# Reciprocal square roots of query and key tiles and of the small norms: a power on GpSimd in place of log and exp on ScalarE

## The chip, the core and the metric

The kernel runs on one core of a Trainium2 chip. A core has a matrix engine (TensorE, in the profile PE for matmuls and PEld for weight loads), VectorE (DVE), ScalarE (ACT), GpSimd (POOL) and SyncE (SP, which here issues the DMAs). Each engine runs its own instructions in order and waits on semaphores for the others. The metric is the device time of one execution in microseconds (us).

## The reference

The program is two blocks of two layers each on 512 tokens of width 1024, in float32. The places that matter here are root-mean-square norms:

```python
def rms_norm(x, g):
    xf = x.astype(jnp.float32)
    y = xf * lax.rsqrt(jnp.mean(xf * xf, axis=-1, keepdims=True) + EPS)   # EPS = 1e-6
    return (y * g.astype(jnp.float32)).astype(x.dtype)

# first block, each layer: L = 16 meta tokens + 512 tokens, 16 query heads, 2 key/value heads of 64
h = rms_norm(x, norm_g)
z = h @ w_in                                     # aq, ak, av, ag, mq, mk, mv, mi, mf, mo, mgate
q = rms_norm(aq.reshape(B, L, 16, 64), q_norm_g) # the query and key norms
k = rms_norm(ak.reshape(B, L, 2, 64), k_norm_g)
q, k = apply_partial_rope(q, cos, sin), apply_partial_rope(k, cos, sin)
ya = sliding_window_sink_attention(q, k, v, sink) * silu(ag)
hm = rms_norm(mlstm_chunkwise(...), out_norm_g)  # per head of 256: the small norm "hsc"
y = concatenate([ya, hm * sigmoid(mo) * silu(mgate)]) @ w_out
x = x + y

# second block, each layer
o_a = rmsnorm(diff_attention(...)) * (1.0 - lam_init)   # per head of 128: "dnorm"
mem_n = rmsnorm(mem, g_mem)                             # "memprep"
...
return rmsnorm(x, g_final)                              # after both layers: "final"
```

## The kernel before

Activations are held transposed, channels on the 128 partitions and the 528 (first block) or 512 tokens along the free dimension. Every projection is a float32 product made of three passes (high x high, high x low, low x high parts). ScalarE rounds each incoming weight piece to its high part (`ch<-st`), VectorE subtracts to get the low part (`cl<-st,ch`).

The order of all work is written out by hand. Class `Order` makes one list of steps (`put(kind, ...)`), and each engine's program walks that list and does its part of every step it knows. So the order of steps in the list is the order of instructions on every engine. Semaphores stand between them: `then_inc(name, keys)` publishes keys, `wait_ge(keys)` waits for them.

The query and key norm is done for nine tiles per layer of the first block, 128 channels (two heads) by 528 tokens each: tile 8 holds the keys, tiles 0 to 7 the queries. A tile goes through these steps:

- projection (`proj`, TensorE), then `qkev` (ScalarE): a copy to the buffer QF and a square to `sq`.
- `qkn`: TensorE multiplies the squares with a block matrix of 1/64, which leaves the mean square of each head on all its partitions (`ps<-sq,cst`). The result lies in the PSUM banks 4 and 5, called P2, which the transposes of the attention probabilities (`sB`, in the profile `ps<-cst,ZR` and `ps<-cst,Z`) use too. ScalarE takes the logarithm with EPS as bias out of P2 into the buffer RS (and so frees P2), then the exponential of -0.5 times it, in place. VectorE scales QF by RS and the gain.
- `rope`: TensorE multiplies QF with the rotation matrix (`ps<-Z,cst`), VectorE multiplies this with the sines, GpSimd multiplies QF with the cosines, VectorE adds both; ScalarE copies the sum into the high part QH, VectorE subtracts to get the low part QL.

`Order.block1` sets where these steps stand. `chain()` puts the `rope` of the tiles in `st["turn"]` and then the `qkn` of those in `st["norm"]`. It is called after a query projection and after each step of filler work. After the keys (8), the values and tiles 0 and 1, the attention loop runs over 32 steps s: scores and softmax `sA(s)`, one unit of filler (`mv`, `cv` or a query projection), `chain()`, transposes `sB(s-1)`, product with the values `sC(s-2)`. Query tiles come in pairs: (2, 3) at s = 4 and 5, (4, 5) at 12 and 13, (6, 7) at 20 and 21; tile t is first needed at s = 4t.

The small norms take a logarithm and an exponential on ScalarE too, over 2 to 32 columns: `hsc` for each of 4 heads per layer (128x5), `memprep` (128x2) and `dnorm` (128x32) once per layer of the second block, `final` (128x4) at the end. The four big norms between the layers (`nrm0`) have the same two functions. ScalarE loads a table before a logarithm and another before the next exponential; copies, squares, tanh and exp go with the latter.

Of the kernel before, what the change touches and what calls it, by code (L numbers as in the profile page):

```python
# [9 lines left out]
ALU = mybir.AluOpType  # L10
ACT = mybir.ActivationFunctionType
X = mybir.AxisListType.X

L = 528
ZC = 25720
NM = 16
EPS = 1e-6
# [11 lines left out]
    ("g1", 8), ("g2", 8), ("gm", 8), ("og", 8), ("qg", 1), ("kg", 1), ("sink", 16), ("cb", 8), ("cw", 32),  # L29
    ("bi", 1), ("bf", 1))]  # L30
DERIVED = [(f"{n}_{l}", w) for n, w in (("negsink", 16), ("qg8", 1), ("og4", 8), ("cwh", 32), ("cbh", 8))
           for l in range(2)] + [("lam", 4), ("eps", 1)]
ENGINES = ("pe", "dve", "act", "pool")


# [101 lines left out]
def v2(ap):  # L137
    return ap.rearrange("p (a b) -> p a b", a=2)
# [131 lines left out]
class Order:  # L270
# [6 lines left out]
    def put(self, *step):  # L277
        self.o.append(step)
# [79 lines left out]
    def block1(self, l):  # L358
# [9 lines left out]

        def chain():

            for t in st["turn"]:
                put("rope", l, t, self.nsq())
            st["turn"] = []
            for t, s in st["norm"]:
                put("qkn", l, t, s)
                st["turn"].append(t)
            st["norm"] = []

        def qk(t, u):
            self.proj(("q", l, t), nid, L, u, t % 2)  # L380
# [371 lines left out]
def program(nc, I, out):  # L752
    with ExitStack() as ctx:
# [50 lines left out]
        def tok(key, T):  # L804
            return ps2(key)[:, :, 0:HALF] if T == L else ps1(key)[:, 0:T]
# [12 lines left out]
        def P(name, i=0, n=1, p=128):  # L818
            return par[0:p, place[name] + i:place[name] + i + n]
# [581 lines left out]
        def scalar_program(act):  # L1401
# [55 lines left out]
            def qkn(l, t, n):  # L1457
                key, rs = ("n", ("qkn", l, t)), RS[t % 3]
                act.wait_ge(("full", key), ("ones",))
                act.activation(v2(rs), tok(key, L), ACT.Ln, bias=P("eps")).then_inc("act_qkn", ("free", key))  # L1460
                act.wait_ge(("free", key))
                act.activation(rs, rs, ACT.Exp, scale=-0.5).then_inc("act_qkn", ("rs", l, t))

            def rope(l, t, n):
                if t < 8:
# [131 lines left out]
                act.wait_ge(("full", key), *sqw(n))  # L1597
                act.activation(v2(sq[n % 2]), tok(key, L), ACT.Tanh, scale=0.5).then_inc("act_tanh", ("ggt", l, k))

            def hsc(l, h):  # L1600
                act.wait_ge(("mss", l, h, 4))
                act.activation(ssq[:, :, h], ssq[:, :, h], ACT.Ln, bias=P("eps"), scale=1.0 / 256).then_inc(
                    "act_hsc", ("hs0", l, h))
                act.wait_ge(("hs0", l, h))
                act.activation(ssq[:, :, h], ssq[:, :, h], ACT.Exp, scale=-0.5).then_inc("act_hsc", ("hss", l, h))

            def ys(l, k):
                y, hi, lo = y_of(k)
                act.wait_ge(("yag", l, k) if k < 8 else ("ym", l, k - 8), ("full", ("gg", l, 7)))
# [2 lines left out]
            def memprep(l):  # L1612
                act.wait_ge(("mem", l))
                for a in range(2):
                    m = act.activation(mem_sq[l][:, a, :], mem_in[l][:, a, :], ACT.Square, accum_out=sm[:, a:a + 1])
                m.then_inc("act_mem", ("ms0", l))
                act.wait_ge(("ms0", l))
                act.activation(sm, sm, ACT.Ln, bias=P("eps"), scale=1.0 / 1024).then_inc("act_mem", ("ms1", l))
                act.wait_ge(("ms1", l))
                act.activation(sm, sm, ACT.Exp, scale=-0.5).then_inc("act_mem", ("memr", l))  # L1620

            def memturn(l):
                act.wait_ge(("memt", l))
# [44 lines left out]
            def dC(l, x, n):  # L1668
# [4 lines left out]
                act.activation(sq[n % 2][:, 0:128], ps1(key)[:, 0:128], ACT.Square,  # L1673
                               accum_out=ss[:, 8 * i + h:8 * i + h + 1]).then_inc(
                    "act_do", ("free", key), ("sqfree", n), ("dss", l, x))

            def dnorm(l):
                act.wait_ge(("dss", l, 31))
                act.activation(ss, ss, ACT.Ln, bias=P("eps"), scale=1.0 / 128).then_inc("act_dnorm", ("ds0", l))
                act.wait_ge(("ds0", l))  # L1680
                act.activation(ss, ss, ACT.Exp, scale=-0.5).then_inc("act_dnorm", ("dsr", l))

            def lqev(l, g, x, t):
                if x == 0:
# [122 lines left out]
                    act.activation(osq_tmp[:, 0:n], OT2[:, a, o:o + n], ACT.Square,  # L1807
                                   accum_out=so[:, 4 * k + a:4 * k + a + 1]).then_inc("act_out", ("osq", k, a))

            def final():  # L1810
                act.wait_ge(("so",))
                act.activation(so[:, 8:12], so[:, 8:12], ACT.Ln, bias=P("eps"), scale=1.0 / 1024).then_inc(
                    "act_out", ("so1",))
                act.wait_ge(("so1",))
                act.activation(so[:, 8:12], so[:, 8:12], ACT.Exp, scale=-0.5).then_inc("act_out", ("so2",))

            do = dict(w=w, sqa=sqa, nrm0=nrm0, nrm=nrm, prep=prep, lines=lines, tab=tab, qkev=qkev, qkn=qkn, rope=rope, swap=swap, vev=vev,
                      vtr=vtr, cvev=cvev, conv=conv, mvev=mvev, agev=agev, m_s=m_s, sA=sA, sB=sB, sC=sC, gr=gr,
                      grf=grf, grt=grt, mA=mA, mB=mB, goev=goev, ggev=ggev, hsc=hsc, ys=ys, memprep=memprep,
                      memturn=memturn, kvvev=kvvev, dqkev=dqkev, dvev=dvev, dgev=dgev, dA=dA, dB=dB, dC=dC,  # L1820
                      dnorm=dnorm, lqev=lqev, lvev=lvev, lS=lS, lse0=lse0, mqev=mqev, lse1=lse1, lgev=lgev, eT=eT,
                      eP=eP, yasp=yasp, fA=fA, fB=fB, mgev=mgev, gtev=gtev, ybs=ybs, yms=yms, mgs=mgs, turn=turn,
                      osq=osq, final=final, bar=act.bar)
            for kind, *a in steps:
                if kind in do:
                    do[kind](*a)
# [1 line left out]
        def vector_program(dve):  # L1828
# [4 lines left out]

            def load():
                dve.memset(ones[:, :], 1.0 / 1024)
                dve.memset(P("eps"), EPS).then_inc("dve_ones", ("ones",))

            def xt(k):
# [544 lines left out]
        def gpsimd_program(pool):  # L2383
            def nrm(nid, k, n):
                if k % 2:
                    T = L if nid < 2 else 512
                    pool.wait_ge(("hh", nid, k))
                    pool.tensor_tensor(hl[:, k, 0:T], sq[n % 2][:, 0:T], hh[:, k, 0:T].bitcast(F32), ALU.subtract).then_inc(
                        "pool_hl", ("hl", nid, k), ("sqfree", n))

            def rope(l, t, n):
                pool.wait_ge(("full", ("rope", l, t)), ("qkn", l, t))
                pool.tensor_tensor(QF[t % 3], QF[t % 3], COS, ALU.mult).then_inc("pool_rope", ("ropec", l, t))

            def vtr(l, g):
                pool.wait_ge(("line",), *bars(("b1", l)))
                pool.memset(VS.bitcast(F32), 0.0)
                pool.memset(zr(7040, 512).bitcast(F32), 0.0).then_inc("pool_ones", ("zero", l))

            def mvones(l):  # L2400
                pool.wait_ge(*bars(("b1", l)))
                if l:
                    pool.wait_ge(*[("tout", x) for x in range(6, 10)])
                pool.memset(MV[:, :, :, 256:258], 1.0).then_inc("pool_ones", ("mvones", l))

            def pn(l, g, i):
                if g == 2:
                    x0, ap = 16 * g + 4 * i, PD[g][:, i, :, 0:128]
                    pool.wait_ge(("lfw", l))
                    pool.tensor_tensor(ap, ap, grow(fd[:, x0:x0 + 4], 128), ALU.mult).then_inc("pool_pn", ("pn", l, g, i))  # L2410

            do = dict(nrm=nrm, rope=rope, vtr=vtr, mvones=mvones, pn=pn, bar=pool.bar)
            for kind, *a in steps:
                if kind in do:
                    do[kind](*a)
# [273 lines left out]
```

## Time and profile before

| | |
|---|---|
| median of 3 runs | 3568.85 us (3568.02 to 3573.87) |
| profiled execution | 3568.43 us, span 3566.6 us |
| mean granted TensorE clock | 0.949 |
| TensorE busy (matmuls) | 3306.8 us, 93% |
| VectorE / ScalarE / GpSimd busy | 43% / 36% / 2% |
| table loads on ScalarE | 79, 101.4 us |
| the chain that ended last | TensorE 58%, VectorE 6%, ScalarE 2% |

The busy shares say that TensorE carries the time; what the others do counts where TensorE, or the end of the program, waits for them. In the rows, the first number of a timeline is the start in us from the beginning of the span. Nearly all instructions have the line of a helper: L91 matmul, L94 transpose, L97 a ScalarE pass, L100 an operation on two tensors, L104 with a scalar, L108 with both, L124 reciprocal. Tiles are told by name: `ps` is PSUM, `Z` and `ZR` the big SBUF buffer, `sq` the squares, `cst` constants, `par` the parameter columns (EPS among them), `stat` the small statistics.

### The profile page before, as it was taken

To read this page: it belongs to the slowest core of one execution; us is meant where nothing else is said; L and a number is where in the kernel's file an instruction comes from. 1 tells how busy PE (TensorE), PEld (TensorE's weight loads), DVE (VectorE), ACT (ScalarE), POOL (GpSimd) and SP (SyncE) were. 2 spreads that over 40 slices of the span, in tenths; PEclk is the share of its full clock that TensorE was granted. 3 is DMA by queue.
4 is the path that set the end of the run, shared out by engine and by line. 5 is a ranking of instruction groups with operands and counts; after the bars stand their busy time and mean duration, and the time that the engine had idled before them with its cause. 6 is when DMAs were issued, how large, how long until landed. Compare 5 with 4: busy or idle time off the path is not lost.

```text
span 3566.6 us, 45061 instructions
## 1 busy us (share of the span) xinstructions
PE 3306.8 (93%) x18614; PEld 2754.0 (77%) x18614; DVE 1545.6 (43%) x3064; ACT 1301.6 (36%) x2668; POOL 60.8 (2%) x52
## 2 busy tenths in 40 slices
PE   6899999878899998899999999999899999998998
PEld 5788777857788688887678877787777688877886
DVE  3565534325565344435542245433435532254333
ACT  3555323335554233334432233223334422233223
POOL 0000000000000000000000000000000000000000
PEclk8999989989999799999999999999999999999999
DMA  2111112241111112322122211233321131212322
GB/s 91 48 41 44 60 36 60 63 147 51 36 48 48 36 60 72 110 88 63 53 95 71 71 60 60 83 95 101 104 88 57 48 106 60 71 48 83 94 90 77
DMA packets 69503, 251.13 MB, mean 70 GB/s; under 512 B 7657, under 2 KB 9577, under 8 KB 68786
## 3 DMA queue, kind: packets, MB, share of 16 engines
q1 hardware_dynamic: 69298, 248.24, 22.2%
q8 instruction: 147, 2.41, 0.3%
q14 instruction: 58, 0.48, 0.0%
HBM read 237.05 MB, written 11.16 MB: 70 GB/s over the span
## 4 chain that ended last, share of the span: by engine, by line
PE 58%; DVE 6%; ACT 2%; issue 1%; DMA 0%; DVEq 0%; ACTq 0%
PE ps L91 56%; PE ps L94 2%; ACT ch L97 1%; DVE cl L100 1%; DVE Z L108 1%; DVE Z L100 1%; DVE ZR L100 1%; DVE Z L118 1%; DVE Z L104 0%; ACT Z L97 0%; DVE Z L111 0%; ACT L97 0%; DMA st<-in_stream_dram 0%; DVE stat L100 0%; DVE Z L124 0%
## 5 line engine op out<-in xcount | busy, mean ns | idle before, releaser
L100 DVE TENSOR_TENSOR cl<-st,ch 128x1024 fp32r<-128x1024 f32 x404 | 494.1, 1227 | 1025.4 <-ACT ch L97 1025.3
L91 PE MATMUL ps<-hh,ch 128*128 128x264 f32 (+1 forms) x2944 | 883.7, 345 | 40.1 <-ACT Z L97 10.3
L91 PE MATMUL ps<-hl,ch 128*128 128x264 f32 (+1 forms) x2944 | 867.8, 340 | 14.9 <-DVE ZR L100 14.9
L91 PE MATMUL ps<-hh,cl 128*128 128x264 f32 (+1 forms) x2944 | 864.9, 338 | 0.0
L97 ACT ACTIVATE ch<-st 128x1024 fp32r<-128x1024 f32 x404 | 426.2, 1058 | 856.2 <-PE ps L91 852.8
L91 PEld LDWEIGHTS ps<-hh,ch 128*128 128x128 f32 x2944 | 510.7, 192 | 135.4 <-issue 30.0
L91 PEld LDWEIGHTS ps<-hl,ch 128*128 128x128 f32 x2944 | 512.6, 193 | 75.2 <-issue 12.1
L91 PEld LDWEIGHTS ps<-hh,cl 128*128 128x128 f32 x2944 | 510.0, 192 | 59.3
L91 PE MATMUL ps<-Z 128*128 128x128 f32 (+9 forms) x1820 | 434.6, 381 | 35.4 <-DVE Z L118 17.0
L97 ACT ACTIVATE Z<-ps 128x512 f32<-128x512 f32 (+6 forms) x558 | 239.7, 441 | 576.5 <-PE ps L91 459.2
L91 PE MATMUL ps<-ZR,ch 128*128 128x512 f32 (+2 forms) x1408 | 378.2, 352 | 4.9 <-DVE Z L108 2.4
L91 PEld LDWEIGHTS ps<-Z 128*128 128x128 f32 (+4 forms) x1820 | 263.7, 198 | 124.0 <-issue 78.2
L91 PE MATMUL ps<-ch,hh 128*128 128x256 f32 (+2 forms) x992 | 320.6, 323 | 1.6 <-DVE sq L100 1.6
L91 PE MATMUL ps<-cl,hh 128*128 128x256 f32 (+2 forms) x992 | 312.3, 315 | 0.0
L91 PE MATMUL ps<-ch,hl 128*128 128x256 f32 (+2 forms) x992 | 311.9, 314 | 0.0
L91 PEld LDWEIGHTS ps<-ZR,ch 128*128 128x128 f32 x1408 | 246.4, 191 | 46.6 <-issue 7.4
L91 PEld LDWEIGHTS ps<-ch,hh 128*128 128x128 f32 (+2 forms) x992 | 218.8, 221 | 26.4 <-issue 17.3
L91 PEld LDWEIGHTS ps<-cl,hh 128*128 128x128 f32 (+2 forms) x992 | 218.2, 220 | 2.0
L91 PEld LDWEIGHTS ps<-ch,hl 128*128 128x128 f32 (+2 forms) x992 | 217.7, 219 | 1.9
L94 PE MATMUL ps<-cst,Z 128*128 128x128 f32 (+3 forms) x974 | 162.2, 287 | 37.9 <-DVE Z L108 19.0
L97 ACT ACTIVATE Z<-Z,stat 128x512 f32<-128x512 f32 (+3 forms) x224 | 131.2, 587 | 180.2 <-DVE stat L104 180.2
L118 DVE COPY Z<-ps 128x512 f32<-128x512 f32 (+7 forms) x156 | 83.2, 541 | 222.9 <-PE ps L91 187.7
(121 smaller groups left out, 2890.7 us busy)
## 6 DMA issues: line engine op xcount, KB each, us to landing
st<-in_stream_dram SPq DMA_DIRECT2D x404, 512.0 KB, 3.5
Z<-bias_tables SPq DMA_DIRECT2D x16, 448.0 KB, 3.5
ya_spill<-Z SPq DMA_DIRECT2D x8, 512.0 KB, 4.0
Z<-ya_spill SPq DMA_DIRECT2D x2, 2048.0 KB, 7.6
Z<-bias_lines SPq DMA_DIRECT2D x8, 448.0 KB, 4.7
bias_tables<-Z SPq DMA_DIRECT2D x8, 448.0 KB, 5.2
Z<-in_x_dram SPq DMA_DIRECT2D x4, 512.0 KB, 4.9
Z<-in_mem_dram SPq DMA_DIRECT2D x2, 1024.0 KB, 5.2
```

What stands on the lines that cost most here:

```text
L91: return Ins(self, self.e and self.e.matmul(o, a, b, start=start, stop=stop, skip_group_check=True))
L94: return Ins(self, self.e and self.e.transpose(o, a, i))
L97: return Ins(self, self.e and self.e.activation(o, i, f, **kw))
L100: return Ins(self, self.e and self.e.tensor_tensor(o, a, b, op))
L108: return Ins(self, self.e and self.e.scalar_tensor_tensor(out=o, in0=a, scalar=s, in1=b, op0=op0, op1=op1))
L118: return Ins(self, self.e and self.e.tensor_copy(o, i))
```

## The change

ScalarE no longer takes the logarithm and exponential of the query and key tiles and of the small norms; GpSimd raises to the power -0.5, with a column `mhalf` of -0.5 as the second operand, broadcast. For the big tiles ScalarE's pass out of PSUM stays as an `Identity` that adds EPS. For the small norms two GpSimd instructions do it, one for the factor 1/n and EPS and one for the power. `nrm0` stays as it was. `chain()` puts `qkn` ahead of the `rope` of the tiles that were already waiting.

```diff
 DERIVED = [...]
-           for l in range(2)] + [("lam", 4), ("eps", 1)]
+           for l in range(2)] + [("lam", 4), ("eps", 1), ("mhalf", 1)]
...
         def chain():
 
-            for t in st["turn"]:
-                put("rope", l, t, self.nsq())
-            st["turn"] = []
+            ready, st["turn"] = st["turn"], []
             for t, s in st["norm"]:
                 put("qkn", l, t, s)
                 st["turn"].append(t)
             st["norm"] = []
+            for t in ready:
+                put("rope", l, t, self.nsq())
...
             def qkn(l, t, n):
                 key, rs = ("n", ("qkn", l, t)), RS[t % 3]
                 act.wait_ge(("full", key), ("ones",))
-                act.activation(v2(rs), tok(key, L), ACT.Ln, bias=P("eps")).then_inc("act_qkn", ("free", key))
-                act.wait_ge(("free", key))
-                act.activation(rs, rs, ACT.Exp, scale=-0.5).then_inc("act_qkn", ("rs", l, t))
+                act.activation(v2(rs), tok(key, L), ACT.Identity, bias=P("eps")).then_inc(
+                    "act_qkn", ("free", key), ("ms", l, t))
...
-            def hsc(l, h):
-                act.wait_ge(("mss", l, h, 4))
-                act.activation(ssq[:, :, h], ssq[:, :, h], ACT.Ln, bias=P("eps"), scale=1.0 / 256).then_inc(
-                    "act_hsc", ("hs0", l, h))
-                act.wait_ge(("hs0", l, h))
-                act.activation(ssq[:, :, h], ssq[:, :, h], ACT.Exp, scale=-0.5).then_inc("act_hsc", ("hss", l, h))
...
                 dve.memset(ones[:, :], 1.0 / 1024)
+                dve.memset(P("mhalf"), -0.5)
...
+            def rsqrt(ap, n, *keys):
+                pool.tensor_scalar(ap, ap, 1.0 / n, EPS, ALU.mult, ALU.add).then_inc("pool_pow")
+                pool.wait_ge(pool.newest, ("ones",))
+                pool.tensor_tensor(ap, ap, P("mhalf").to_broadcast(list(ap.shape)), ALU.pow).then_inc("pool_pow", *keys)
+
+            def qkn(l, t, n):
+                rs = RS[t % 3]
+                pool.wait_ge(("ms", l, t), ("ones",))
+                pool.tensor_tensor(rs, rs, P("mhalf").to_broadcast([128, L]), ALU.pow).then_inc("pool_pow", ("rs", l, t))
+
+            def hsc(l, h):
+                pool.wait_ge(("mss", l, h, 4))
+                rsqrt(ssq[:, :, h], 256, ("hss", l, h))
...
+            def final():
+                pool.wait_ge(("so",))
+                rsqrt(so[:, 8:12], 1024, ("so2",))
```

`memprep` (1/1024), `dnorm` (1/128) and `final` lose the same pair on ScalarE and get the same `rsqrt` on GpSimd.

TensorE, in the attention loop where the statistics of tile 3 and the rotation of tile 2 meet (`ps<-sq,cst` is `qkn`, `ps<-Z,cst` is `rope`, `ps<-cst,ZR` the next transposes):

```order
 L91 MATMUL ps<-ch,hl 16x256
+L91 MATMUL ps<-sq,cst 128x264 [waits act_qk,dve_pt]
+L91 MATMUL ps<-sq,cst 128x264
 L91 MATMUL ps<-Z,cst 128x264 [waits dve_qkn,act_rows,act_ya]
 L91 MATMUL ps<-Z,cst 128x264
-L91 MATMUL ps<-sq,cst 128x264 [waits act_qk,dve_pt]
-L91 MATMUL ps<-sq,cst 128x264
 L94 MATMUL ps<-cst,ZR 80x128 [waits dve_smax,act_qkn]
```

The statistics go ahead of the rotation, and the transposes follow the rotation.

ScalarE at the same place (`Z<-ps,par` is the pass of `qkn` out of PSUM, `ZR<-Z` the copy of `rope`, `ZR<-ps 80x256` the high part of the transposed probabilities):

```order
 L97 ACTIVATE Z<-ps 16x256 [waits pe_proj]
+L97 ACTIVATE Z<-ps,par 128x528 [waits pe_qkn]
 L97 ACTIVATE ZR<-Z 128x528 [waits dve_rope]
-L97 ACT_TABLE_LOAD
-L97 ACTIVATE Z<-ps,par 128x528 [waits pe_qkn]
-L97 ACT_TABLE_LOAD
-L97 ACTIVATE Z<-Z 128x528 [waits act_qkn]
 L97 ACTIVATE ZR<-ps 80x256 [waits pe_turn]
```

Five instructions become two, and the pass no longer stands behind the copy that waits for the rotation.

GpSimd in the first layer, from the keys to the last query pair (`Z<-Z,par` is the power, `Z<-Z,cst` the product with the cosines):

```order
+L100 TENSOR_TENSOR Z<-Z,par 128x528 [waits dve_ones,act_qkn]
 L100 TENSOR_TENSOR Z<-Z,cst 128x528 [waits dve_qkn,pe_rope]
 L127 MEMSET ZR 128x128 [waits act_prep,dve_prep,pool_hl,pe_sums,d_line]
 L127 MEMSET ZR 128x512
+L100 TENSOR_TENSOR Z<-Z,par 128x528 [waits act_qkn]
 L127 MEMSET Z 128x20x2
-L100 TENSOR_TENSOR Z<-Z,cst 128x528 [waits dve_qkn,pe_rope] x8
+L100 TENSOR_TENSOR Z<-Z,par 128x528 [waits act_qkn]
+L100 TENSOR_TENSOR Z<-Z,cst 128x528 [waits dve_qkn,pe_rope] x2
+L100 TENSOR_TENSOR Z<-Z,par 128x528 [waits act_qkn] x2
+L100 TENSOR_TENSOR Z<-Z,cst 128x528 [waits dve_qkn,pe_rope] x2
```

Each pair of tiles now has its two powers ahead of its two products; the last two rows come twice more. On VectorE the scale of tile 3 likewise stands ahead of the rotation of tile 2 and waits for GpSimd instead of ScalarE.

## Rows read from the trace of the kernel before

**Rows 1.** Waits of TensorE: for whom, us in total, times, the longest.
```profile
PE ps L94 <- ACT Z L97: 38.3, 12, 4.1
```

**Rows 2.** Timeline of TensorE, tiles 2 and 3: start, us, work, count, [idle before <-releaser].
```profile
151.12 1.05 PE L91 MATMUL ps<-sq,cst 128*128 128x264 f32 x4
154.50 0.44 PE L94 MATMUL ps<-cst,ZR 128*80 128x128 f32 x1 [2.33 <-ACT Z L97]
...
161.67 1.13 PE L91 MATMUL ps<-Z,cst 128*128 128x264 f32 x4 [0.51 <-issue]
162.64 1.05 PE L91 MATMUL ps<-sq,cst 128*128 128x264 f32 x4
167.75 0.31 PE L94 MATMUL ps<-cst,ZR 128*80 128x128 f32 x1 [4.05 <-ACT Z L97]
...
174.96 1.13 PE L91 MATMUL ps<-Z,cst 128*128 128x264 f32 x4 [0.52 <-issue]
```

**Rows 3.** Timeline of ScalarE around `qkn`; last, its group of table loads.
```profile
90.08 1.28 ACT L97 ACT_TABLE_LOAD   x1
...
152.46 1.28 ACT L97 ACT_TABLE_LOAD   x1
153.75 0.70 ACT L97 ACTIVATE Z<-ps,par 128x528 f32<-128x528 f32 x1
...
155.76 0.64 ACT L97 ACTIVATE Z<-Z 128x528 f32<-128x528 f32 x1
...
165.03 0.64 ACT L97 ACTIVATE ZR<-Z 128x528 fp32r<-128x528 f32 x1 [3.46 <-DVE Z L100]
...
166.99 0.70 ACT L97 ACTIVATE Z<-ps,par 128x528 f32<-128x528 f32 x1
...
799.63 1.28 ACT L97 ACT_TABLE_LOAD   x1
...
L97 ACT ACT_TABLE_LOAD x79 | 101.4, 1283 | 2.1 <-PEq L2677 0.7
```

**Rows 4.** Timeline of TensorE at the other waits.
```profile
69.72 3.17 PE L91 MATMUL ps<-Z 33*20 33x512 f32 x4 [3.44 <-ACT Z L97]
...
95.33 1.16 PE L91 MATMUL ps<-Z,cst 128*128 128x264 f32 x4 [2.90 <-ACT Z L97]
...
104.28 1.13 PE L91 MATMUL ps<-Z,cst 128*128 128x264 f32 x4 [2.45 <-DVE Z L108]
...
641.01 0.78 PE L91 MATMUL ps<-hl,ch 128*128 128x264 f32 x2 [5.77 <-DVE ZR L100]
...
804.53 1.13 PE L91 MATMUL ps<-Z,cst 128*128 128x264 f32 x4
```

**Rows 5.** Timeline of ScalarE, final norm: first and last instruction.
```profile
3555.27 1.28 ACT L97 ACT_TABLE_LOAD   x1
...
3558.18 0.21 ACT L97 ACTIVATE stat<-stat 128x4 f32<-128x4 f32 x1
```

**Rows 6.** Groups by shape, GpSimd, then VectorE: count | busy us, mean ns | idle before.
```profile
L100 POOL TENSOR_TENSOR Z<-Z,cst 128x528 f32<-128x528 f32 x18 | 23.5, 1306 | 513.3 <-PE ps L91 513.3
...
L127 POOL MEMSET Z<- 128x40 f32 x2 | 0.3, 140 | 0.0
...
L100 DVE TENSOR_TENSOR ZR<-ps,ZR 128x512 fp32r<-128x512 f32 x50 | 34.4, 688 | 12.2 <-ACT ZR L97 11.8
...
L108 DVE SCALAR_TENSOR_TENSOR Z<-Z,par 128x528 f32<-128x528 f32 x18 | 13.8, 769 | 53.3 <-ACT Z L97 53.3
...
L100 DVE TENSOR_TENSOR sq<-ps,cst 128x528 f32<-128x528 f32 x18 | 12.7, 708 | 33.5 <-PE ps L91 33.5
...
L124 DVE RECIPROCAL Z<-Z 4x512 f32<-4x512 f32 x2 | 6.7, 3342 | 0.1
```

**Rows 7.** Timelines of GpSimd and VectorE where both subtract.
```profile
1502.18 1.30 POOL L100 TENSOR_TENSOR hl<-sq,hh 128x512 fp32r<-128x512 f32 x1 [8.80 <-ACT hh L97]
...
1502.93 1.10 DVE L100 TENSOR_TENSOR hl<-sq,hh 128x512 fp32r<-128x512 f32 x1 [0.83 <-ACT hh L97]
```

More of the change, by code:

```diff
@@ L1616, in memprep @@
                 m.then_inc("act_mem", ("ms0", l))
[L1617 to L1620, printed above, removed]
             def memturn(l):
@@ L1675, in dC @@
                     "act_do", ("free", key), ("sqfree", n), ("dss", l, x))
[L1677 to L1681, printed above, removed]
             def lqev(l, g, x, t):
@@ L1808, in osq @@
                                    accum_out=so[:, 4 * k + a:4 * k + a + 1]).then_inc("act_out", ("osq", k, a))
[L1810 to L1815, printed above, removed]
             do = dict(w=w, sqa=sqa, nrm0=nrm0, nrm=nrm, prep=prep, lines=lines, tab=tab, qkev=qkev, qkn=qkn, rope=rope, swap=swap, vev=vev,
                       vtr=vtr, cvev=cvev, conv=conv, mvev=mvev, agev=agev, m_s=m_s, sA=sA, sB=sB, sC=sC, gr=gr,
-                      grf=grf, grt=grt, mA=mA, mB=mB, goev=goev, ggev=ggev, hsc=hsc, ys=ys, memprep=memprep,
+                      grf=grf, grt=grt, mA=mA, mB=mB, goev=goev, ggev=ggev, ys=ys, memprep=memprep,
                       memturn=memturn, kvvev=kvvev, dqkev=dqkev, dvev=dvev, dgev=dgev, dA=dA, dB=dB, dC=dC,
-                      dnorm=dnorm, lqev=lqev, lvev=lvev, lS=lS, lse0=lse0, mqev=mqev, lse1=lse1, lgev=lgev, eT=eT,
+                      lqev=lqev, lvev=lvev, lS=lS, lse0=lse0, mqev=mqev, lse1=lse1, lgev=lgev, eT=eT,
                       eP=eP, yasp=yasp, fA=fA, fB=fB, mgev=mgev, gtev=gtev, ybs=ybs, yms=yms, mgs=mgs, turn=turn,
-                      osq=osq, final=final, bar=act.bar)
+                      osq=osq, bar=act.bar)
             for kind, *a in steps:
@@ L2410, in pn, with memprep, dnorm @@
                     pool.tensor_tensor(ap, ap, grow(fd[:, x0:x0 + 4], 128), ALU.mult).then_inc("pool_pn", ("pn", l, g, i))
-            do = dict(nrm=nrm, rope=rope, vtr=vtr, mvones=mvones, pn=pn, bar=pool.bar)
+            def rsqrt(ap, n, *keys):
[9 more added lines that the diff above has]
+                rsqrt(ssq[:, :, h], 256, ("hss", l, h))
+            def memprep(l):
+                pool.wait_ge(("ms0", l))
+                rsqrt(sm, 1024, ("memr", l))
+            def dnorm(l):
+                pool.wait_ge(("dss", l, 31))
+                rsqrt(ss, 128, ("dsr", l))
+            def final():
+                pool.wait_ge(("so",))
+                rsqrt(so[:, 8:12], 1024, ("so2",))
+            do = dict(qkn=qkn, hsc=hsc, memprep=memprep, dnorm=dnorm, final=final, nrm=nrm, rope=rope, vtr=vtr, mvones=mvones, pn=pn, bar=pool.bar)
             for kind, *a in steps:
```

## The prediction

> **What bounds the kernel now.** Read the page's table of engines first: TensorE is busy 93% of the span and every other engine under half, so a microsecond counts only where TensorE stands still. Next the waits of TensorE by releaser: the largest group, 38.3 us in 12 waits, is transposes held up by a ScalarE pass [rows 1]. The timeline says which. One pair of query tiles (2 and 3) of the attention loop stands in [rows 2]. After the statistics matmuls of tile 2 (`ps<-sq,cst`, 151.12) the transposes of the probabilities start only at 154.50, after 2.33 us of idleness; after those of tile 3 (162.64) only at 167.75, after 4.05 us. Both need the pair of banks P2, which the logarithm pass of `qkn` still reads. ScalarE's timeline shows why it is late [rows 3]: for tile 2 a table load of 1.28 us stands ahead of the logarithm (152.46, 153.75 + 0.70 = 154.45); for tile 3 ScalarE first sits until 165.03 in front of the `rope` copy of tile 2, then loads, and the logarithm ends at 167.69. Six such pairs (three per layer) make 6 x (2.33 + 4.05) = 38.3 us, the whole group. The other places where these functions hold TensorE up [rows 4]: the bias-line matmuls (3.44 us, first layer only), the rotation matmuls of tiles 0 and 1 (2.90 and 2.45; both come again in the second layer), and the first output projection behind the last head's norm (5.77, in both layers). After the last matmul the end of the program runs through the final norm's logarithm and exponential [rows 5].
>
> **What is removed, added and moved.** ScalarE loses the logarithm and exponential of 18 big tiles and of 13 small norms (8 `hsc`, 2 `memprep`, 2 `dnorm`, 1 `final`): 31 times two table loads, so 62 of 79 loads go [rows 3], 62 x 1.283 = 79.5 us of ScalarE, most of it beside work. What stays for a big tile is one pass with a bias, priced like the logarithm (0.70 us). GpSimd gets 18 powers over 128x528 and 26 small instructions. Moved: `qkn` now stands ahead of `rope` on all engines.
>
> The power has no row in this trace. Call its time over 128x528 X. From below: GpSimd's multiplication of the same shape, 1.31 us [rows 6]; a power is not cheaper, as it reads the same operands. From above, the only iterated function here is VectorE's reciprocal, 3.34 us for 512 columns against 0.69 for an ordinary pass [rows 6], 4.8 times; applied to GpSimd that is 6.3 us, an estimate. A software logarithm and exponential could be dearer still; that is a rival. I take the geometric middle of the two ends, X = 2.9 us: GpSimd gives no reason to prefer either.
>
> **The sum, with X = 2.9.**
> - First wait of a pair: the pass starts at 152.46 where the load started and ends 153.16; the wait is 1.04 in place of 2.33. Saved 1.29 x 6 = 7.7 us.
> - Second wait: TensorE reaches the place 1.29 earlier, and the statistics of tile 3 come first: 160.38 to 161.4. The pass ends at 162.15, while the rotation matmuls of tile 2 keep TensorE busy until 162.4. Nothing is left of 4.05: 24.3 us in six.
> - What is late next there: the power of tile 3 ends at 162.15 + X; behind it in VectorE's queue stand the scale 0.77, two rotation passes of 0.71, ScalarE's copy 0.64, the low part 0.71 and the low part of the transposed probabilities 0.69 [rows 3, 6], which frees P2 for the next transposes: with 0.25 us of hand-overs 166.6 + X. TensorE gets there after the rotation of tile 3, in before 174.96 + 0.98 [rows 2], now 170.6. So the cover holds up to X = 4.0. Beyond it each us is lost; from X of about 4.5 twice, since tile 2's power then also delays, through VectorE and ScalarE's exponentials of the next scores, the pass of tile 3: a loss of 0.5 + 2(X - 4.5) per pair (estimate).
> - Tile 0: the load started at 90.08 [rows 3], so the pass ends at 90.79 and the scale at 91.6 + X = 94.5. TensorE finished its projection at 92.43 [rows 4] and has the statistics of tile 1 (1.05) to do first: it waits 1.0 in place of 2.90. 1.9 x 2 = 3.8 us.
> - Tile 1: the pass ends about 94.2, the scale 97.9; TensorE is there at about 99.9: 2.45 x 2 = 4.9 us.
> - Bias lines: ScalarE's evacuations come after two loads and the exponential (2.57 + 0.64): 3.2 us, once.
> - Last head: the same load, logarithm, load, exponential as at the end, 3.12 us [rows 5], become two small GpSimd instructions. No row has them; from both sides 0.3 us (two fills of 40 columns at 0.14, [rows 6]) and 2 x 1.31 = 2.6 us (two passes as long as those over 528 columns), which is still under 3.12; dearer only in rival 1. I take 1.0 with hand-overs, nearer to the short rows as the tiles have 2 to 32 columns: saved 2.1 x 2 = 4.2 us; the copies of the gated tiles no longer stand behind the loads.
> - Final norm: 3555.27 to 3558.39 [rows 5] becomes 1.0: 2.1 us, all on the end path. The other small norms wait beside projections: nothing, and if their cover is gone no more than these 2.1 each.
> - Tile 8: in the first layer hidden behind the bias lines and tile 0's projection up to about X = 10 (estimate); in the second its load stood at 799.63 [rows 3], so the scale is ready at 801.2 + X, and TensorE needs it at 804.53 [rows 4]: hidden up to X = 3.3.
>
> Together 50.2 us. TensorE then runs closer to VectorE and ScalarE, and short waits of under a microsecond will grow, so I book 85%: 43 us. The profiled execution took 3568.43 us (span 3566.6), within 0.5 us of the median 3568.85: 3526 us.
>
> **Two rules of the Trainium skill.** The load rows read 1.28 us, and the next pass begins 0.01 us after a load ends [rows 3]. The page ScalarE: Activation LUTs (What ACT_TABLE_LOAD costs) gives the same 1283 ns for the load but adds a drain of about 1380 ns to every switch, 2.66 us in all; by that the whole first wait of 2.33 would go, 6 us more over six pairs. The trace shows no such gap, so this stays out of the sum.
>
> GpSimd's subtraction of 1502.18 to 1503.48 overlaps a VectorE subtraction of two SBUF operands that begins at 1502.93 and takes 1.10 where others take 0.69: it ends 0.55 after GpSimd does [rows 7]. The page SBUF — State Buffer (SBUF: two separate sides) says that the port pair shared by the two is "an exclusive lock, not a bandwidth split". The trace agrees.
>
> **The rivals.**
> 1. *The power is slow, and the loss comes through VectorE.* VectorE waits in order for the power with the softmax reductions of the next step and the weight splits behind it, GpSimd's own rotation product stands behind the next tile's power, and TensorE waits for both. Per pair 5.34 is saved and 0.5 + 2(X - 4.5) lost: the pairs turn at about X = 6.9. At X = 13 (ten multiplications): pairs 6 x (5.34 - 17.5) = -73; tile 0 waits 11.2 for 2.90, -17 in two; tile 1 about 7.5 for 2.45, -10; tile 8 first layer 3.0, second 9.7, -13; lines, last heads and end +9.5. Sum -103: 3671 us. For it: a power takes many arithmetic steps where a multiplication takes one, and even that costs GpSimd 1.8 times VectorE's. Against it: nothing in the trace; the row that would tell is missing.
> 2. *It comes out even.* X between about 6.3 and 7.5: at 6.3 the pairs save 1.2 each (7.4), tiles 0, 1 and 8 lose 3, the rest saves 9.5: 14 us, 3554; at 7.5 the pairs lose 1.2 each and tiles 0, 1 and 8 some 9: 3575.
> 3. *The port decides.* X is small, but every power holds VectorE's passes over two SBUF operands for its length, or waits for a weight split of 1.23 us in front of it: 18 x 1.23 = 22 us given back, 3548. Against it: at a pair VectorE mostly stands waiting for the power itself.
>
> **How the numbers follow.** A measurement tells 0.2%, 7 us, from no change. My forecast (X up to 5): 0.42, with a range of its own from 3513 (X = 1.31, nothing given back, the small norms at their lower end) to 3550. The port: 0.05. X from 5 up to the even case, still faster: 0.06. Even: 0.06 within 0.2%. Slow power: 0.41; within it the time rises about 17 us per us of X. So faster 0.53, same 0.06, slower 0.41. The range goes from 3513 up to 3655, X = 12; what lies above is part of the slow case and some 0.15.
>
> **What would show it.** Right: GpSimd's group `Z<-Z,par` 128x528, 18 times, under 4 us each; ScalarE with 17 table loads; the wait of TensorE at the first transposes of a pair about 1.0 and at the second none; nothing longer than 1 us at the third. Wrong: that group over 7 us, `VectorE <- GpSimd` as a wait of more than 60 us in total, and waits of TensorE for VectorE at the next transposes (rival 1); or short powers with VectorE's weight splits stretched from 1.23 us (rival 3).

## The result: 5014.9 us, 40% slower

The changed kernel takes 5014.89 us (median of 4 runs, 5011.99 to 5016.57) against 3568.43 before (median of four; three of the four runs stand in the table above with 3568.85), a ratio of 1.405 with a 95% interval of 1.402 to 1.407. The prediction (3526, range 3513 to 3655) had the wrong sign, and the measured time lies far outside its range. Its rival 1, the slow power, is what happened, at a size that it did not consider.

The page of the changed kernel. After the engines' totals come tenths of busy time in 40 slices of the span; PEclk is the clock granted to TensorE, in tenths of full speed:

```profile
span 5011.8 us, 45013 instructions
PE 3318.7 (66%) x18614; PEld 2760.0 (55%) x18614; DVE 1559.0 (31%) x3065; ACT 1203.1 (24%) x2562; POOL 1612.3 (32%) x96
PE   3131404079982040404299999999999899999998
POOL 5968595920007959595800000000000000000000
PEclk7566757588996575757588999999999999999999
```

TensorE does the same 18614 matmuls in nearly the same time (3318.7 us, 3306.8 before); its idle time grew from 259.8 to 1693.1 us. The slices in which it idles are those in which GpSimd works: the query and key tiles of the two layers of the first block. One group of instructions explains them. First that group on GpSimd (busy, mean ns of one, idle before it), with the small powers; then the waits of VectorE, TensorE and ScalarE (us in total, times, longest):

```profile
L100 POOL TENSOR_TENSOR Z<-Z,par 128x528 f32<-128x528 f32 x18 | 1526.6, 84814 | 357.6 <-ACT Z L97 357.6
L100 POOL TENSOR_TENSOR stat<-stat,par 128x32 f32<-128x32 f32 x2 | 10.8, 5411 | 0.2
L100 POOL TENSOR_TENSOR stat<-stat,par 128x5 f32<-128x5 f32 x8 | 9.3, 1166 | 0.7
L100 POOL TENSOR_TENSOR stat<-stat,par 128x4 f32<-128x4 f32 x1 | 1.0, 1008 | 0.1
```

```profile
DVE Z L108 <- POOL Z L100: 1510.7, 18, 84.6
PE ps L91 <- DVE sq L100: 675.1, 10, 84.7
PE ps L91 <- DVE ZR L100: 503.9, 14, 81.1
PE ps L91 <- DVE Z L108: 357.5, 26, 84.2
PE ps L94 <- ACT Z L97: 5.4, 6, 0.9
ACT ZR L97 <- DVE Z L100: 894.1, 16, 169.5
```

A power over 128x528 takes 84.8 us, 65 times the multiplication of the same shape [rows 6]. VectorE waits for nearly all of each (1510.7 of 1526.6 us), and TensorE for VectorE. The wait of [rows 1] did shrink as predicted, from 38.3 to 5.4 us, and so did the end of the program [rows 5]: scale and power of the final norm take 0.20 and 1.01 us for the 3.12 before, and VectorE's wait for them falls from 2.90 to 1.41 us. Beside the loss these gains are small.

The timeline of one pair shows how it is passed on (start, us, what; in brackets the idle time before it and who ended it):

```profile
389.72 85.06 POOL L100 TENSOR_TENSOR Z<-Z,par 128x528 f32<-128x528 f32 x1 [44.79 <-ACT Z L97]
474.82 0.77 DVE L108 SCALAR_TENSOR_TENSOR Z<-Z,par 128x528 f32<-128x528 f32 x1 [84.51 <-POOL Z L100]
475.50 0.42 DVE L100 TENSOR_TENSOR ZR<-ps,ZR 128x256 fp32r<-128x256 f32 x1
475.98 2.13 PE L91 MATMUL ps<-sq,cst 128*128 128x264 f32 x4 [81.09 <-DVE ZR L100]
478.69 1.46 DVE L104 TENSOR_SCALAR Z<-Z,stat 128x272 f32<-128x272 f32 x2
478.92 84.61 POOL L100 TENSOR_TENSOR Z<-Z,par 128x528 f32<-128x528 f32 x1 [4.13 <-ACT Z L97]
...
563.50 1.30 POOL L100 TENSOR_TENSOR Z<-Z,cst 128x528 f32<-128x528 f32 x1
563.57 1.79 DVE L108 SCALAR_TENSOR_TENSOR Z<-Z,par 128x528 f32<-128x528 f32 x1 [82.97 <-POOL Z L100]
565.28 0.69 DVE L100 TENSOR_TENSOR sq<-ps,cst 128x528 f32<-128x528 f32 x1
566.03 1.22 PE L91 MATMUL ps<-ZR 80*128 80x256 f32 x4 [84.38 <-DVE sq L100]
```

The first power of the pair holds the scale, and behind the scale the low part `ZR<-ps,ZR` that TensorE needs before the next tile's statistics. That tile's power cannot start until these are done: it starts 4.13 us after the first has ended, and TensorE stands still for 81.09 us of the first and, for the rotation pass `sq<-ps,cst` behind the scale, 84.38 us of the second. That pass frees the banks of the next scores. (Two powers could not overlap in any case, as both run on GpSimd; what is missing is work for TensorE beside them.) The statistics behind the long wait take 2.13 us, where they took 1.05 before [rows 2]: from 476 to 480 us the granted clock is 0.50, the lower of TensorE's two levels (1.2 of 2.4 GHz), after 81 us without work.

### The profile page after: what moved, and what is told of

It reads as the page before. It is cut to its first block and busy times, and to the rows that moved or that the text cites. A ratio compares the mean times of both kernels' runs of the same rounds, so it can differ in the third digit from the quotient of the medians.

```text
span 5011.8 us, 45013 instructions
## 1 busy us (share of the span) xinstructions
PE 3318.7 (66%) x18614; PEld 2760.0 (55%) x18614; DVE 1559.0 (31%) x3065; ACT 1203.1 (24%) x2562; POOL 1612.3 (32%) x96
## 5 line engine op out<-in xcount | busy, mean ns | idle before, releaser
L100 POOL TENSOR_TENSOR Z<-Z,par 128x528 f32<-128x528 f32 x18 | 1526.6, 84814 | 357.6 <-ACT Z L97 357.6
L91 PE MATMUL ps<-hh,ch 128*128 128x264 f32 (+1 forms) x2944 | 885.9, 345 | 40.4 <-ACT Z L97 10.6
L91 PEld LDWEIGHTS ps<-hh,ch 128*128 128x128 f32 x2944 | 512.4, 193 | 136.6 <-issue 30.2
L108 DVE SCALAR_TENSOR_TENSOR Z<-Z,par 128x528 f32<-128x528 f32 (+3 forms) x66 | 60.6, 918 | 1526.8 <-POOL Z L100 1510.7
L91 PE MATMUL ps<-ZR 128*128 128x256 f32 (+3 forms) x784 | 108.6, 316 | 507.9 <-DVE sq L100 507.0
L91 PEld LDWEIGHTS ps<-ZR 64*128 64x128 f32 (+2 forms) x784 | 82.9, 197 | 525.1 <-DVE sq L100 511.2
L91 PE MATMUL ps<-sq,cst 128*128 128x264 f32 x72 | 25.4, 486 | 486.5 <-DVE ZR L100 486.5
```

The lines of the kernel that those rows point to most:

```text
L91: return Ins(self, self.e and self.e.matmul(o, a, b, start=start, stop=stop, skip_group_check=True))
L100: return Ins(self, self.e and self.e.tensor_tensor(o, a, b, op))
L108: return Ins(self, self.e and self.e.scalar_tensor_tensor(out=o, in0=a, scalar=s, in1=b, op0=op0, op1=op1))
```

## The experiments

Theory A: the power over 128x528 is the whole loss, and the other parts gain about what the sum said. The rivals blamed the small powers (B), the new order (C) or the port (D); F and G are about whether short powers are hidden, H (experiments 9 to 12) about which pass holds TensorE up when they are not. All times are medians (experiment 8 is a single run). The experiments ran in three batches, each on another chip, with the kernel before run beside them (3563.8 us for experiments 1 to 4, 3564.2 for 5 to 8, 3566.7 for 9 to 12); every ratio is against the "before" of its batch, with its 95% interval. "Idle time" is TensorE's in the profiled run: the span less its busy time, both from the page.

**1. The small norms alone.** `qkn` keeps logarithm and exponential, and the order is that of before. The edit, in the changed kernel (`chain` too is put back):

```diff
-                act.activation(v2(rs), tok(key, L), ACT.Identity, bias=P("eps")).then_inc(
-                    "act_qkn", ("free", key), ("ms", l, t))
+                act.activation(v2(rs), tok(key, L), ACT.Ln, bias=P("eps")).then_inc("act_qkn", ("free", key))
+                act.wait_ge(("free", key))
+                act.activation(rs, rs, ACT.Exp, scale=-0.5).then_inc("act_qkn", ("rs", l, t))
```

> Only the 13 small norms become powers on GpSimd; the 18 big tiles keep logarithm and exponential on ScalarE, and the order is that of before. Theory A (all of the loss is the power over 128x528; the other parts gain about what the sum said): last heads 2 x (3.12 - 1.45) = 3.3 and the final norm 1.8 less, 3563 us, at most 3558 if the 26 loads that go had held something else up. Theory B (the small powers, of which the one over 128x32 takes 5.4 us, stand on the path too): 3570 or more.

3563.1 us, ratio 0.999 (0.998 to 1.001). No difference that can be told. The interval runs from 8 us less to 4 us more: the 5 us of A lie in it, and a loss that would count beside the 1446 us does not. The trace shows a small gain: TensorE's waits for `ZR` of VectorE, the last heads' among them, are 17.0 us where they were 19.4, and the end of the program is shortened as in the changed kernel.

**2. The order alone.** The edit, in the kernel before (experiment 4 is its reverse, in the changed kernel):

```diff
-            for t in st["turn"]:
-                put("rope", l, t, self.nsq())
-            st["turn"] = []
+            ready, st["turn"] = st["turn"], []
             for t, s in st["norm"]:
                 put("qkn", l, t, s)
                 st["turn"].append(t)
             st["norm"] = []
+            for t in ready:
+                put("rope", l, t, self.nsq())
```

> Only the order: the norm of a tile stands ahead of the rotation of the tile before it, on every engine; logarithm and exponential stay on ScalarE, no power anywhere. Theory A: the second wait of a pair (4.05 us, six times) goes or nearly goes, since the logarithm no longer stands behind ScalarE's rotation copy, so about 20 us less: 3548. Theory C (the new order itself holds the rotation of the first tile back behind the norm of the second and so takes part in the loss): 3575 or more.

3555.1 us, ratio 0.997 (0.996 to 0.999): a gain, so C is out as a loss, but under half of A's 20 us. TensorE's waits in this kernel:

```profile
PE ps L91 <- DVE sq L100: 22.5, 10, 2.9
PE ps L94 <- ACT Z L97: 18.8, 12, 2.3
```

The wait at the transposes fell by 19.5 us, and a new one stands at the scores, for `sq<-ps,cst` (1.6 us in 2 in the kernel before). The two nearly cancel: idle time is 256.9 us, where it was 259.8. The timeline says why:

```profile
165.34 0.77 DVE L108 SCALAR_TENSOR_TENSOR Z<-Z,par 128x528 f32<-128x528 f32 x1 [2.55 <-ACT Z L97]
166.03 0.70 DVE L100 TENSOR_TENSOR sq<-ps,cst 128x528 f32<-128x528 f32 x1
166.78 0.74 PE L91 MATMUL ps<-ZR 80*128 80x256 f32 x4 [2.52 <-DVE sq L100]
```

In the new order VectorE waits 2.55 us for the scale of tile 3, with the rotation pass of tile 2, whose matmuls have long ended, behind it. The prediction did not see this wait.

**3. A multiplication in place of the power.** In GpSimd's `qkn`:

```diff
-                pool.tensor_tensor(rs, rs, P("mhalf").to_broadcast([128, L]), ALU.pow).then_inc("pool_pow", ("rs", l, t))
+                pool.tensor_tensor(rs, rs, P("mhalf").to_broadcast([128, L]), ALU.mult).then_inc("pool_pow", ("rs", l, t))
```

> The changed kernel with a multiplication in place of each of the 18 powers over 128x528 on GpSimd, everything else as changed (the tiles are then scaled by a wrong factor). Same operands, queue and waits, about 1.31 us each. Theory A: the time is that of the sum at X = 1.31, between 3513 (nothing given back) and 3522. Theory C: the order or the small norms carry part of the loss, and it stays above 3568. Theory D (GpSimd's passes hold VectorE's through the shared port): about 3545.

3520.6 us, ratio 0.987 (0.984 to 0.990), where the sum said 3513 to 3522. Only the operation differs from the changed kernel, and 1494 us go with it: A. The number is right, its parts less so. TensorE's waits in this kernel, with what answers to [rows 1]:

```profile
PE ps L91 <- DVE sq L100: 23.7, 11, 2.8
PE ps L94 <- ACT Z L97: 5.4, 6, 0.9
```

32.9 us of the old wait went (the prediction's 32.0), but the wait for `sq` gave back 22. Idle time fell by 30.2 us in all (259.8 to 229.6). In the profiled run another 27.5 us came from TensorE being busy for less, 3279.3 for 3306.8 us with the same matmuls and the granted clock at 0.959 for 0.949. That run was the fastest of four (3510.7). So of the 43 us between the medians some 30 are waits. The sum had 50.2; less the 22 that the wait for `sq` takes back it would have had 28. The rest is likely the clock, which the sum did not have in it, and so it is in part luck that 3520.6 lies where the sum put it.

**4. Powers, with the order of before.**

> The changed kernel with the order of before: powers on GpSimd, the rotation of a tile ahead of the norm of the next. Theory A: every power is serial either way, 18 x 84.8 us: 5015 us, less or more by at most 40. Theory C: with the rotation product ahead of the next power on GpSimd a good part of the loss goes, 4900 or under.

5030.4 us, ratio 1.410 (1.405 to 1.414), within A's range and 15 above the changed kernel. The order is not the cause.

**5 to 7. How much of a power is hidden?** The power over the first 24, 64 or 128 columns only; the other columns of each tile are left as they are. With 24:

```diff
-                pool.tensor_tensor(rs, rs, P("mhalf").to_broadcast([128, L]), ALU.pow).then_inc("pool_pow", ("rs", l, t))
+                pool.tensor_tensor(rs[:, 0:24], rs[:, 0:24], P("mhalf").to_broadcast([128, 24]), ALU.pow).then_inc("pool_pow", ("rs", l, t))
```

> The changed kernel with each of the 18 powers over the first 24 columns only (the other 504 are left out, their tiles are scaled wrongly). From the small powers seen (0.38 us + 0.16 us per column) X is about 4.2. Theory F (the prediction's cover: a pair hides a power up to 4.0 us): within 8 us of the kernel with multiplications, 3520 to 3530. Theory G (no cover: every power lies on the path from its first microsecond, as (5014.9 - 3520.6) / (84.8 - 1.3) = 17.9 us for each us of X on a straight line): 3520.6 + 17.9 x 2.9 = 3572.

> As before with 64 columns, X about 10.6. Theory F: 17 us for each us of X below the 3671 at X = 13, so 3630. Theory G: 3520.6 + 17.9 x 9.3 = 3687.

> As before with 128 columns, X about 20.9. Theory F: 3671 + 17 x 7.9 = 3805. Theory G: 3520.6 + 17.9 x 19.6 = 3871.

| columns | X, us | time, us | us per us of X since the row above | idle time, us | idle us per us of X | F | G |
|---|---|---|---|---|---|---|---|
| 528, multiplied | 1.34 | 3520.6 | | 229.6 | | | |
| 24 | 4.43 | 3570.0 | 16.0 | 265.9 | 11.7 | 3520 to 3530 | 3572 |
| 64 | 10.73 | 3678.1 | 17.2 | 362.9 | 15.4 | 3630 | 3687 |
| 128 | 20.92 | 3863.5 | 18.2 | 549.0 | 18.3 | 3805 | 3871 |
| 528 | 84.8 | 5014.9 | 18.0 | 1693.1 | 17.9 | | |

X is the mean of the power's group in each profile. Of the two theories G holds for the time: a power costs it nearly what it lasts, 18 times. The idle time tells more. Of the first 3.1 us of X it takes 11.7 us per us, so about a third of that step is hidden from it, and only from 64 columns on all 18 powers stand in it in full. The rest of the first step in the profiled runs, 20.3 us, is TensorE being busy for longer (3279.3 and 3299.6 us, granted clock 0.959 and 0.950). The first slope is also the least certain: its two kernels ran in different batches, and the intervals of their ratios alone allow 12 to 20 us per us (estimate). At 24 columns the kernel is already no faster than before (ratio 1.001, 1.000 to 1.003), although X is within the prediction's cover of 4.0 but for 0.4 us. Where the cover was thought to be stands this (24 columns):

```profile
160.20 4.23 POOL L100 TENSOR_TENSOR Z<-Z,par 128x24 f32<-128x24 f32 x1 [4.04 <-ACT Z L97]
164.40 1.29 POOL L100 TENSOR_TENSOR Z<-Z,cst 128x528 f32<-128x528 f32 x1
164.46 1.79 DVE L108 SCALAR_TENSOR_TENSOR Z<-Z,par 128x528 f32<-128x528 f32 x1 [3.32 <-POOL Z L100]
166.17 0.69 DVE L100 TENSOR_TENSOR sq<-ps,cst 128x528 f32<-128x528 f32 x1
166.92 1.22 PE L91 MATMUL ps<-ZR 80*128 80x256 f32 x4 [5.50 <-DVE sq L100]
```

The scale is stretched as well, from 0.77 [rows 6] to 1.79 us, as GpSimd's rotation product runs beside it: the same overlap as in [rows 7], about 1 us a pair.

Behind this wait TensorE is slower as well. Its granted clock in the 6 us behind the 5.50 us of idleness, and in the same stretch of experiments 3 and 12, where no wait of that length stands; the rows are those of experiments 5, 3 and 12 (stretch, length, busy time and instructions, clock, DMA):

```profile
167.00:173.00 6.00, 6.00 (x35) 0.65 0.00 0
167.00:173.00 6.00, 6.00 (x53) 1.00 0.01 1
167.00:173.00 6.00, 6.00 (x53) 1.00 0.01 4
```

From 167 to 171 us it is 0.50, the lower level, and in the six microseconds TensorE does 35 matmuls against 53 (not all of one size).

**8. The power by itself.** At the end of the kernel with the small norms, on constant data, powers of other shapes, each behind the last (`tt` waits for the instruction before and issues the next, `a_` holds 1.3, `mh` is the broadcast exponent, `e_` a full tile of it). Then comes one over 256 columns with the exponent 1, and last a power over 528 columns while VectorE runs, eight times over, a product of two SBUF operands over 512 columns, a scaling over 256 and a copy over 384:

```diff
+                tt(b_, a_, mh(128, 528), ALU.pow)
+                tt(b_, a_, e_, ALU.pow)
+                tt(b_[0:16], a_[0:16], mh(16, 528), ALU.pow)
+                tt(b_[:, 0:1], a_[:, 0:1], mh(128, 1), ALU.pow)
+                tt(b_[:, 0:264], a_[:, 0:264], mh(128, 264), ALU.pow)
```

> The kernel with only the small norms on GpSimd, and at its end, on constant data, GpSimd powers of other shapes, and then one over 128x528 while VectorE runs passes with two SBUF operands over 512 columns, scalings and copies, one after the other. Theory A (the power is a loop over the columns that costs 0.16 us for each, whatever stands in it): 84.8 us for 128x528 with a broadcast or a full exponent, the same for 16 partitions, 42.6 for 264 columns, 41 for 256 columns with exponent 1, 0.54 for one column. Rival (its time depends on the number of elements, or on the values): 16 partitions take about 11, exponent 1 well under 41. The port: VectorE's passes take their usual time (0.69 for 512 columns) beside the power if it gives the port back between columns; if a GpSimd instruction holds it from its start to its end, the first of them waits for about 84.

The groups, and from the timeline the power with the full tile as exponent (start, us):

```profile
L100 POOL TENSOR_TENSOR Z<-Z,par 128x528 f32<-128x528 f32 x2 | 170.6, 85303 | 0.2
3642.84 84.68 POOL L100 TENSOR_TENSOR Z<-Z 128x528 f32<-128x528 f32 x1
L100 POOL TENSOR_TENSOR Z<-Z,par 16x528 f32<-16x528 f32 x1 | 84.6, 84614 | 0.1
L100 POOL TENSOR_TENSOR Z<-Z,par 128x264 f32<-128x264 f32 x1 | 42.5, 42460 | 0.1
L100 POOL TENSOR_TENSOR Z<-Z 128x256 f32<-128x256 f32 x1 | 41.1, 41141 | 0.1
L100 POOL TENSOR_TENSOR Z<-Z,par 128x1 f32<-128x1 f32 x1 | 0.5, 549 | 0.1
```

The time follows the columns alone: 16 partitions take as long as 128, half the columns half as long, and an exponent of 1 (the row of 256 columns) is no cheaper. From the rows of 1 and 264 columns: (42460 - 549) / 263 = 159 ns a column, and 0.39 us once. Theory A's price by columns holds; the rival is out for the partition counts and exponents tried. VectorE beside a power over 528 columns that runs from 3897.95 to 3983.07:

```profile
3897.91 0.69 DVE L100 TENSOR_TENSOR Z<-Z 128x512 f32<-128x512 f32 x1 [332.45 <-POOL Z L100]
3898.64 1.04 DVE L105 TENSOR_SCALAR Z<-Z 128x256 f32<-128x256 f32 x1
3899.71 0.36 DVE L118 COPY Z<-Z 128x384 f32<-128x384 f32 x1
3900.11 0.69 DVE L100 TENSOR_TENSOR Z<-Z 128x512 f32<-128x512 f32 x1
3900.83 0.29 DVE L105 TENSOR_SCALAR Z<-Z 128x256 f32<-128x256 f32 x1
```

One scaling is stretched, from 0.29 to 1.04 us, until 1.7 us into the power; the other 23 passes, the last of them ending at 3910.2, all repeat the times shown. That is 12.3 us into the power; beside its last 73 us no pass of VectorE runs, here or in the changed kernel, so nothing is shown of them. The same shows in the changed kernel at 478.69, where two scalings take 1.46 us together as the power starts at 478.92; in the kernel with 24 columns a power that starts beside the same two (at 160.20) leaves them at 0.63. And it grows with the columns: a scale that begins together with a power takes 0.79 us at 24 columns, 0.85 at 64, 0.96 at 128 and 1.63 at 528. So the disturbance belongs to the start of a long power. Rival 3's "every power holds VectorE's passes for its length" is out.

**9 and 10. Can the cover be had?** The kernel with 24 columns again, with the steps swapped in one engine's list: on VectorE alone (9), on VectorE and GpSimd (10):

```diff
-            for kind, *a in steps:
+            mine = list(steps)
+            for j in range(len(mine) - 1):
+                if mine[j][0] == "qkn" and mine[j + 1][0] == "rope":
+                    mine[j:j + 2] = mine[j + 1], mine[j]
+            for kind, *a in mine:
```

> The kernel with powers over 24 columns (the rest of each tile left out, as there), and on VectorE alone the rotation of a tile stands ahead of the scale of the next again; the other engines keep the new order. Theory H (a power of 4.4 us finds no cover because the rotation pass that frees TensorE's banks stands behind the scale that waits for it): TensorE's waits for that pass fall from 42.5 us in 10 to about 10, and the time from 3570 to about 3545. Theory G (a power is on the path whatever the order on VectorE): 3565 to 3575.

> As the last, and on GpSimd too the rotation product stands ahead of the next power, which so starts up to 2 us later. Theory H: VectorE's third rotation pass no longer waits for the power through GpSimd's queue, 3535 to 3540. Theory G: 3565 to 3575.

3555.6 us (ratio 0.998, 0.996 to 1.000) and 3545.1 us (0.995, 0.993 to 0.997), from 3570.0 (1.001). The waits for `sq`, 42.5 us in 10, are 3.6 in 5 and 3.2 in 4, but only 14 and 25 us of the time went with them (12 and 23 by the ratios), against the 25 and 30 to 35 of theory H. Idle time fell from 265.9 to 255.4 and 246.2, where the multiplication has 229.6: the two swaps together bring back about half of what the short powers cost. The other half moved on: TensorE's waits for ScalarE's `Z` are 48.1 us in 21 in kernel 9 and 38.7 in 19 in kernel 10, where they were 19.4 in 17 without the swap. The exponentials are late because the maxima (`stat<-ps`) too stand behind the scale on VectorE, as the timeline of kernel 10 shows:

```profile
163.26 0.77 DVE L108 SCALAR_TENSOR_TENSOR Z<-Z,par 128x528 f32<-128x528 f32 x1 [1.92 <-POOL Z L100]
164.55 0.71 DVE L121 TENSOR_REDUCE stat<-ps 128x2 f32<-128x544 f32 x1
165.49 0.49 ACT L97 ACTIVATE Z<-ps,stat 128x272 f32<-128x272 f32 x1 [3.70 <-DVE stat L100]
```

**11 and 12. A version without the large powers.** One ScalarE pass in place of two, small norms on GpSimd, the new order; in 12 with VectorE's swap of experiment 9. The edit of the pass, against the kernel before:

```diff
-                act.activation(v2(rs), tok(key, L), ACT.Ln, bias=P("eps")).then_inc("act_qkn", ("free", key))
-                act.wait_ge(("free", key))
-                act.activation(rs, rs, ACT.Exp, scale=-0.5).then_inc("act_qkn", ("rs", l, t))
+                act.activation(v2(rs), tok(key, L), ACT.Abs_reciprocal_sqrt, bias=P("eps")).then_inc(
+                    "act_qkn", ("free", key), ("rs", l, t))
```

> A version without the large powers: one ScalarE pass (absolute reciprocal square root) in place of logarithm and exponential for the 18 big tiles, small norms on GpSimd, the new order. The load in front of the pass stays, the second load is no longer ahead of the scale, which comes 1.28 + 0.65 = 1.9 us earlier than with the order alone (3555). Theory H (the scale's lateness is what TensorE pays at the rotation pass): about 10 x 1.9 less, 3536. Rival (the two loads of each tile stay, and ScalarE pays the second one at its next exponential, on the path of the scores): 3550 to 3555.

> As the last, with the rotation of a tile ahead of the scale of the next on VectorE alone. Theory H: TensorE's waits for the rotation pass (22.5 us in 10 with the order alone) fall to under 10 us; 3530. Rival (the scale is now late for the next tile instead): 3540 or more.

3522.7 us (ratio 0.989, 0.986 to 0.992) and 3513.1 us (0.986, 0.983 to 0.989): 12 is 53.6 us faster than before and the fastest of the kernels that compute every norm. Both beat their forecasts of 3536 and 3530. The rival of 11 is out. The waits for `sq` fell to 10.9 us in 11 and 3.4 in 12 (forecast: under 10). Of the 53.3 us between the profiled runs of 12 and of the kernel before, 34.3 are idle time (225.5 for 259.8) and 19.0 busy time (3287.8 for 3306.8, granted clock 0.957 for 0.949). The load for the next exponentials now comes behind the pass and the rotation copy, off the way to the scale; in 12:

```profile
152.68 1.28 ACT L97 ACT_TABLE_LOAD   x1
153.97 0.70 ACT L97 ACTIVATE Z<-ps,par 128x528 f32<-128x528 f32 x1
156.26 0.65 ACT L97 ACTIVATE ZR<-Z 128x528 fp32r<-128x528 f32 x1 [1.59 <-DVE Z L100]
158.11 1.28 ACT L97 ACT_TABLE_LOAD   x1
159.78 0.49 ACT L97 ACTIVATE Z<-ps,stat 128x272 f32<-128x272 f32 x1 [0.39 <-DVE stat L100]
```

The load ends at 159.39, and ScalarE still waits 0.39 us for the maxima after it: it costs nothing there.

## Why the prediction was wrong

- **X, the power over 128x528: the failing term.** Taken 2.9 us between 1.31 and 6.3; it is 84.8. The upper end was scaled from VectorE's reciprocal, another function on another engine. A rival went to 13, and the measured value is 6.5 times that. The sentence "GpSimd gives no reason to prefer either" was an admission that nothing bounded X from above; the range then should not have ended at X = 12. To its credit the slow case had a chance of 0.41, and what lies above the range 0.15.
- **The mechanism of rival 1** (VectorE waits in order, GpSimd's product behind the power, TensorE behind both) is what the trace shows, though the passes that TensorE waited for are others than the reductions and weight splits it named: the low part of the transposed probabilities and the rotation pass. Its slope is right too: forecast 17 us per us of X, measured 17.2 to 18.2 from 24 columns on. The prediction's own formulas with X = 84.8 give: pairs 6 x (5.34 - 0.5 - 2 x 80.3) = -935; tile 0 2 x (2.9 - 83.0) = -160, tile 1 2 x (2.45 - 79.3) = -154, tile 8 -156, the rest +9.5. That is 4964, 51 us under the measured time; 11.9 of the 51 are TensorE being busy for longer than before (3318.7 for 3306.8 us), which the formulas leave out.
- **The cover up to X = 4.0: wrong.** The passes behind the scale were listed, but only the last of them was followed, to the next transposes. The first, `sq<-ps,cst`, is needed at once by the next scores, and with it the wait returned at 1.3 us (22 us, experiment 3). At X = 4.43 the forecast sum would still have said faster by some 37 us (tiles 0 and 8 lose 4.2 of the 50.2 and the pairs 2.6, and 85% are booked); measured is even. So the forecast would have been too low even with the right price: on a straight line between the first two rows of the table X = 2.9 gives 3520.6 + 16.0 x 1.56 = 3546, not 3526 (estimate).
- **First and second wait of a pair: right.** 38.3 became 5.4, the predicted 6 x 1.04 = 6.2.
- **Small norms: right in their rows,** 1.29 us for the final norm (0.20 + 0.08 between + 1.01) against 1.0 taken. VectorE waited 1.5 us less there, not 2.1, as part of the first load before had run beside other work. Their gain on the total (4.2 + 2.1) could not be told from the time (experiment 1).
- **ScalarE's relief:** right (1301.6 to 1203.1 us busy, 17 loads left), and worth little by itself.
- **The port (rival 3):** it exists where a GpSimd pass of ordinary length runs beside VectorE's (0.77 to 1.79 us), not for the length of a power. Its other half, a power that waits for a weight split, is there in eight powers, which begin during a split of 1.23 us and last 85.06 to 85.08 us for 84.61: some 3.6 us together, of the 22 priced. The rule of the Trainium skill that the prediction quotes, an exclusive lock (SBUF — State Buffer, SBUF: two separate sides), fits an ordinary pass and the first 1.7 us of the power, and not the 10.6 us behind them, in which VectorE's passes keep their usual times.
- **The clock: left out of the sum.** The kernel before itself ran between 3549.6 us (granted clock 0.957) and 3575.7 us (0.947) in the 51 runs beside the experiments, 26 us apart, half of the largest gain here. The rows behind experiment 5's timeline show one wait behind which it was lower.

Open: what GpSimd does in the 159 ns of a column, and how much of the gains of experiments 3, 11 and 12 is clock that the shorter waits gave back and how much would differ between runs anyway.

## What to carry to other kernels

An operation that no row of the trace shows has no upper bound: measure it alone, over one column and over many, before it is put on a path, and if that can't be done let the range say so. When a waiting instruction is moved ahead of others on an in-order engine, follow each instruction behind it to its own consumer; the consumer that needs its pass first sets the cover. To shed a table load, first look for one function on the same engine that gives the result in a single pass.

## What the runs showed of the hardware

- GpSimd's power costs 159 ns a column and 0.39 us once, whatever the partitions (16 or 128) and for the exponents -0.5 and 1: 65 times its multiplication over 528 columns.
- A power over 528 columns stretched VectorE's passes only in its first 1.7 us; up to 12.3 us, as far as passes ran beside it, there was nothing more.
- ScalarE's absolute reciprocal square root takes 0.70 us over 128x528 from PSUM, like its logarithm, behind a load of 1.28 us.
- TensorE's busy time moved by 27.5 us with the granted clock (0.949 and 0.959) between two profiled kernels with the same matmuls. It is nearly as large as the waits that were taken away (30.2). After one wait of 5.50 us the clock stood at the lower level (0.50) for the next 4 us.
